# The last pair of experts: both gate-up blocks first, both down blocks second, and the last piece and the prompt outputs in halves

## The reference

```python
def expert_block(args):
    xb, e = args
    h = xb @ w_gu[e] + b_gu[e]
    g = jnp.minimum(h[:, 0::2], SWIGLU_LIMIT)
    up = jnp.clip(h[:, 1::2], -SWIGLU_LIMIT, SWIGLU_LIMIT)
    act = (up + 1.0) * (g * jax.nn.sigmoid(SWIGLU_ALPHA * g))
    return act @ w_dn[e] + b_dn[e]
...
out = jnp.zeros((T + 1, D), x2d.dtype).at[slot_tok].add(ys * slot_gate[:, None])
x = x + f
```

## Time and profile before

| | us |
|---|---|
| median of the runs | 1132.9 |
| profiled execution, its own time | 1134.25 |
| its span, first to last instruction | 1132.3 |
| PE busy | 1076.4 (95%) |
| DVE busy | 323.8 (29%) |
| ACT busy | 152.5 (13%) |
| mean granted clock of PE | 0.977 |

### The profile page before, as it was taken

One profiled execution on the slowest core, in us unless ns is written; L12 is line 12 of the kernel. 1 busy time (PEld: TensorE's weight loads), 2 busy tenths in 40 slices (PEclk: granted clock), 3 DMA queues, 4 the chain that ended last, 5 costly groups with the idle time before them and its releaser, 6 DMA issues.

```text
span 1132.3 us, 12759 instructions
## 1 busy us (share of the span) xinstructions
PE 1076.4 (95%) x4945; PEld 428.5 (38%) x4945; DVE 323.8 (29%) x651; ACT 152.5 (13%) x278; POOL 47.9 (4%) x78
## 2 busy tenths in 40 slices
PE   4999987999999999999999999999999999999996
PEld 3676543333333333333333333333333323333332
DVE  1383438413131313131313131313131221213132
ACT  2143512010101010101010101011110101010100
POOL 4154000000000000000000000000000000000000
PEclk9999977899999999999999999999999999999998
DMA  9905404999999999999999999999999999999991
GB/s 338 376 5 147 175 11 150 359 428 418 427 425 430 427 427 427 429 429 427 428 429 430 426 427 429 430 426 428 430 429 427 428 430 428 427 429 427 428 425 73
DMA packets 32684, 421.51 MB, mean 372 GB/s; under 512 B 4386, under 2 KB 4626, under 8 KB 8062
## 3 DMA queue, kind: packets, MB, share of 16 engines
q1 hardware_dynamic: 31134, 418.08, 88.2%
q0 software_dynamic: 1264, 2.75, 0.7%
q10 hardware_dynamic: 256, 0.26, 0.1%
HBM read 419.81 MB, written 2.33 MB: 373 GB/s over the span
## 4 chain that ended last, share of the span: by engine, by line
PE 74%; DMA 20%; DVE 2%; ACT 2%; issue 1%; SPq 0%; DVEq 0%; ACTq 0%
PE ps L1523 29%; DMA ring<-in_w_gate_up_dram 20%; PE ps L1549 16%; PE ps L1483 9%; PE ps L1171 3%; PE ps L1195 3%; PE ps L1565 3%; PE ps L1531 2%; PE ps L1368 1%; PE ps L1198 1%; PE ps L1500 1%; PE ps L1181 1%; DMA con<-in_const_dram 1%; PE ps L1559 0%; PE ps L1269 0%
## 5 line engine op out<-in xcount | busy, mean ns | idle before, releaser
L1523 PE MATMUL ps<-ring,regA 128*64 128x512 f32 x1536 | 339.2, 595 | 15.0 <-DMA ring<-in_w_gate_up_dram 14.6
L1523 PEld LDWEIGHTS ps<-ring,regA 128*64 128x64 f32 x1536 | 109.8, 137 | 238.7 <-issue 208.8
L1549 PE MATMUL ps<-ring,regA 128*64 128x512 f32 x768 | 174.0, 602 | 0.1
L1121 DVE TENSOR_SCALAR regA<-ps 128x512 f32<-128x512 f32 x32 | 22.1, 692 | 415.8 <-PE ps L1531 415.8
L654 ACT ACTIVATE regA<-regA 128x512 f32<-128x512 f32 x32 | 20.1, 630 | 661.1 <-DVE regA L1121 661.1
L1135 DVE COPY regA<-ps 64x512 f32<-64x512 f32 x64 | 44.1, 689 | 206.5 <-PE ps L1549 205.5
L1483 PE MATMUL ps<-regA 128*128 128x512 f32 (+1 forms) x192 | 97.5, 634 | 2.0 <-DVE regA L1044 2.0
L1549 PEld LDWEIGHTS ps<-ring,regA 128*64 128x64 f32 x768 | 53.2, 138 | 107.2 <-issue 97.7
L1565 PE MATMUL ps<-regA 128*128 128x512 f32 (+1 forms) x136 | 66.6, 613 | 0.0
L1523 PE MATMUL ps<-regX,regA 128*64 128x512 f32 x256 | 57.6, 592 | 0.0
L1523 PE MATMUL ps<-regA 128*64 128x512 f32 x256 | 57.6, 592 | 0.0
(11 more groups left out here) (270 smaller groups left out, 720.3 us busy)
## 6 DMA issues: line engine op xcount, KB each, us to landing
ring<-in_w_gate_up_dram SPq DMA_DIRECT2D x96, 2048.0 KB, 27.9
ring<-in_w_down_dram SPq DMA_DIRECT2D x48, 2048.0 KB, 30.5
regX<-in_w_gate_up_dram SPq DMA_DIRECT2D x16, 2048.0 KB, 26.9
regA<-in_w_gate_up_dram SPq DMA_DIRECT2D x16, 2048.0 KB, 25.7
regA<-in_w_down_dram SPq DMA_DIRECT2D x8, 2048.0 KB, 30.7
regX<-in_w_down_dram SPq DMA_DIRECT2D x8, 2048.0 KB, 32.1
regA<-in_w_in_dram SPq DMA_DIRECT2D x8, 896.0 KB, 14.3
regA<-in_w_out_dram SPq DMA_DIRECT2D x2, 1024.0 KB, 10.5
```

What stands on the lines that cost most here:

```text
L1121: dve.tensor_scalar(g_sb, gu[:, 0::2], LIMIT, None, ALU.min).then_inc(m_g, 1)
L1523: mm = pe.matmul(ps[64 * h:64 * h + 64, 1 + n, :], xT[:, kt, 64 * odd:64 * odd + 64], w[:, c:c + 512], start=(kt == 0), stop=False)
L1549: mm = pe.matmul(ps[64 * n:64 * n + 64, 4, :], actT[:, j, 64 * h:64 * h + 64], w[:, 1024 * j + 512 * n:1024 * j + 512 * n + 512], start=(h ...
```

## The change

In the last pair alone, pieces are loaded and used in another order: the even expert's gate-up (180 to 183), the odd expert's gate-up (184 to 187), the even expert's down (188, 189), the odd expert's down (190, 191). The even expert's down goes to PSUM bank 4 as before; the odd expert's goes to bank 3, and its transposed activation to a tile of its own (`actT_last`, which lies where `g_sb` was). The even expert's result is copied by DVE as soon as its down is done; of the odd expert's result DVE copies one half and ACT the other. The last piece is loaded as two transfers of 1 MB, the second with a semaphore of its own (`s_last`), for which PE waits in the middle of the piece. The two output tiles of `y_prompt` are stored in four halves of 512 columns, each as soon as its add is done. Two semaphores that nobody waited for from another engine are dropped from the list of names.

The diff, cut to its core:

```diff
+        actT_last = g_sb.rearrange("p (j t) -> p j t", j=4)
...
+        LAST_PAIR = [(odd, j) for odd in range(2) for j in range(GU)] + [(odd, GU + h) for odd in range(2) for h in range(2)]
...
-            for i in range(E * PIECES - 2 * SLOTS, E * PIECES):
+            for i in range(E * PIECES - 2 * SLOTS, (E - 2) * PIECES):
                 sp.wait_ge(m_used, i - SLOTS + 1)
                 load_piece(i % SLOTS, i // PIECES, i % PIECES)
+            for i, (odd, j) in enumerate(LAST_PAIR, (E - 2) * PIECES):
+                sp.wait_ge(m_used, i - SLOTS + 1)
+                if i < E * PIECES - 1:
+                    load_piece(i % SLOTS, E - 2 + odd, j)
+                else:
...
+                    sp.dma_start(dst[:, 0:2, :], src[:, 0:2, :]).then_inc(s_slot[i % SLOTS], 16)
+                    sp.dma_start(dst[:, 2:4, :], src[:, 2:4, :]).then_inc(s_last, 16)
...
             for i in range(2):
-                sp.wait_ge(m_add, ADDS * n_over + (done + 6 + 2 * i))
-                sp.sem_inc(sp_passed, 1)
-                sp.dma_start(yp[P * i:P * i + P, :], x_row[:, i, :]).then_inc(s_out, 16)
-            sp.wait_ge(s_out, 16 * 6)
+                for h in range(2):
+                    sp.wait_ge(m_add, ADDS * n_over + (done + 5 + 2 * i + h))
+                    sp.sem_inc(sp_passed, 1)
+                    sp.dma_start(yp[P * i:P * i + P, 512 * h:512 * h + 512],
+                                 x_row[:, i, 512 * h:512 * h + 512]).then_inc(s_out, 16)
+            sp.wait_ge(s_out, 16 * 8)
...
-            pair(PAIRS - 1, False, False)
+            sigmoid(E - 2)
+            copy_act(E - 2)
+            sigmoid(E - 1)
+            copy_act(E - 1, actT_last)
+            act.wait_ge(m_used, PIECES * E)
+            act.activation(y_sb[1][64:128, :], ps[64:128, 3, :], ACT.Copy).then_inc(m_ysb, 1)
...
-            pair(PAIRS - 1, False)
+            activate(E - 2)
+            dve.wait_ge(m_add, ADDS * (PAIRS - 1))
+            add(PAIRS - 1)
+            place_gates(PAIRS - 1)
+            activate(E - 1)
+            dve.wait_ge(m_used, PIECES * E - 2)
+            for n in range(2):
+                dve.tensor_copy(y_sb[n][0:64, :], ps[64 * n:64 * n + 64, 4, :]).then_inc(m_ysb, 1)
+            dve.wait_ge(m_used, PIECES * E)
+            dve.tensor_copy(y_sb[0][64:128, :], ps[0:64, 3, :]).then_inc(m_ysb, 1)
+            dve.wait_ge(m_add, ADDS * PAIRS)
...
+            def down_last(odd, h, lhs, bank):
+
+                w = landed_last(odd, GU + h)
+                for j in range(4):
+                    if odd and h and j == 2:
+                        pe.wait_ge(s_last, 16)
+                    for n in range(2):
+                        mm = pe.matmul(ps[64 * n:64 * n + 64, bank, :], lhs[:, j, 64 * h:64 * h + 64],
+                                       w[:, 1024 * j + 512 * n:1024 * j + 512 * n + 512],
+                                       start=(h == 0 and j == 0), stop=(h == 1 and j == 3))
+                mm.then_inc(m_used, 1)
+
+            def pair_last():
...
+                act_transposes(p * 2)
+                place_half(gated, y_sb, 1, 1).then_inc(m_pl, 1)
+                gate_up(p, 0, 1, False, True)
+                pe.wait_ge(m_aT, p * 2 + 1)
+                pe.wait_ge(m_add, p * ADDS + 4)
+                down_last(0, 0, actT, 4)
+                act_transposes(p * 2 + 1)
+                down_last(0, 1, actT, 4)
+                pe.wait_ge(m_aT, p * 2 + 2)
+                down_last(1, 0, actT_last, 3)
+                down_last(1, 1, actT_last, 3)
...
-            pair(PAIRS - 1, PAIRS // 2 - 1, 2, False)
+            pair_last()
```

More of the change, by code:

```diff
@@ L169, in hybrid_layer, with at_last @@
         slot = [ring[:, s, :] for s in range(6)] + [regA[:, tail - PIECE:tail], regX[:, 0:PIECE]]
+        LAST_PAIR = [(odd, j) for odd in range(2) for j in range(GU)] + [(odd, GU + h) for odd in range(2) for h in range(2)]
+        def at_last(odd, j):
+            return divmod(2 * PIECES + LAST_PAIR.index((odd, j)), SLOTS)
         def at(x, j):
@@ L216, in hybrid_layer @@
         s_zero = sem("zeroed")
+        s_last = sem("last_half_piece_landed")
         s_dve, s_act, s_pool = sem("dve_step"), sem("act_step"), sem("pool_step")
@@ L222, in hybrid_layer @@
                  "sc_t", "sc_cp", "sc_tr", "s_rd", "s_neg", "s_exp", "s_pn", "s_ptr", "s_pcp", "s_pv",
-                 "h_last", "kr_tr", "krow_cp", "st_tr", "st_cp", "out_a", "xmid_a", "out_r", "xq_in", "xq", "xq_tr",
+                 "kr_tr", "krow_cp", "st_tr", "st_cp", "out_a", "xmid_a", "out_r", "xq_in", "xq", "xq_tr",
                  "xq_cp", "xs_rows", "xmid", "wr_g", "ss_f", "ms_f", "rstd_f", "xn",
-                 "xnt_tr", "xnt_cp", "xnt_cp2", "logit", "topd", "tope", "mask", "posd", "placed", "ovd", "gt_tr", "gt_cp")
+                 "xnt_tr", "xnt_cp", "xnt_cp2", "logit", "topd", "tope", "mask", "posd", "ovd", "gt_tr", "gt_cp")
         S = {n: sem(n) for n in names}
@@ L654, in sigmoid, with copy_act @@
                 act.activation(sig_sb, g_sb, ACT.Sigmoid, scale=ALPHA).then_inc(m_sig, 1)
-            def copy_act(q):
+            def copy_act(q, dst=actT):
                 act.wait_ge(m_atr, q + 1)
-                act.activation(actT[:, :, :], ps[:, 3, :].rearrange("p (j t) -> p j t", j=4),
+                act.activation(dst[:, :, :], ps[:, 3, :].rearrange("p (j t) -> p j t", j=4),
                                ACT.Copy).then_inc(m_aT, 1)
@@ L911, in _ @@
             then(dve.tensor_tensor(hs[:, :, NP_:T], rT[:, :, NP_:T], vec[:, :, R_H0:R_H0 + NS], ALU.mult))
-            then(dve.tensor_tensor(hs[:, :, NP_:T], hs[:, :, NP_:T], uT[:, :, NP_:T], ALU.add), "h_last")
+            then(dve.tensor_tensor(hs[:, :, NP_:T], hs[:, :, NP_:T], uT[:, :, NP_:T], ALU.add))
             dve.wait_ge(S["gelu"], 1)
@@ L1008, in places @@
                 then(dve.scalar_tensor_tensor(out=place_cols[r, i, 0:E], in0=ps[r, CBANK[i], 0:E],
-                                              scalar=float(POS0), in1=msk[r, i, :], op0=ALU.add, op1=ALU.mult), "placed")
+                                              scalar=float(POS0), in1=msk[r, i, :], op0=ALU.add, op1=ALU.mult))
             add_r(0, 0, 1)
@@ L1512, in landed, with landed_last, gate_up @@
                 return slot[s]
-            def gate_up(p, r, x, over):
+            def landed_last(odd, j):
+                again, s = at_last(odd, j)
+                pe.wait_ge(s_slot[s], (E // 4 - 1) * 48 + (16 * again + 16))
+                return slot[s]
+            def gate_up(p, r, x, over, last=False):
                 odd = x % 2
@@ L1518, in gate_up @@
                     if kt % 2 == 0:
-                        w = landed(r, x, kt // 2, over)
+                        w = landed_last(odd, kt // 2) if last else landed(r, x, kt // 2, over)
                     for n in range(2):
@@ L1602, in pair @@
                 down(p, r, x + 1, over, ahead)
+            def down_last(odd, h, lhs, bank):
[9 more added lines that the diff above has]
+            def pair_last():
+                p = PAIRS - 1
+                pe.wait_ge(m_xT, p * 2 + 2)
+                gate_up(p, 0, 0, False, True)
+                pe.wait_ge(m_ysb, p * 4)
+                pe.wait_ge(m_gated, p * 2)
+                pe.wait_ge(m_idx, p + 1)
+                place_quarters(gated, y_sb)
+                place_half(gated, y_sb, 0, 0)
+                place_half(gated, y_sb, 0, 1).then_inc(m_pl, 1)
+                place_half(gated, y_sb, 1, 0)
+                act_transposes(p * 2)
[9 more added lines that the diff above has]
+                down_last(1, 1, actT_last, 3)
             def gather_first(g):
```

2 lines of the change are left out of this document (added).

## The result

The changed kernel takes 1128.66 us (median of 6, 1127.07 to 1128.95), the one before beside it 1133.45 (median of 6, 1132.42 to 1136.16): a ratio of 0.995 [0.994, 0.996], faster by about half a per cent. Timed twice more it gave 1129.04 beside 1135.08 (0.995 [0.9937, 0.9962]) and 1128.17 beside 1134.65 (0.9946 [0.993, 0.9963]), so the medians differ by 4.8, 6.0 and 6.5 us. The forecast was 1127.0, a gain of 6.0, with a range from 1124.9 to 1129.0; 1128.66 lies near the range's upper end.

A forecast was written before the change was run, and what follows sets the result against it. The prediction took full DMA engines moving weights as the bound, leaving only work behind the last piece to shorten. 5.65 plus 0.35 made 6.0 off 1132.9, so 1126.9, stated as 1127.0 us; range 1124.9 to 1129.0.

The forecast's parts named there:

- Landings: Loads at the end: the last pieces land as before, piece 190 at 1108.4 and piece 191 at 1113.1 us.
- Products: Last down on PE: 32 products at full clock take 7.09 from 1108.4 to 1115.5, 6.4 us less than 1121.94.
- The branch: PE's branch past the overflow loop, uncovered behind the last half piece: 3.49 us, delaying placing and taking back 1.5.
- Rival A: Branch past the overflow loop stays covered: placing begins at 1116.45, 1.5 more gained, 1125.4 us; chance 0.22.
- The clock: PE's clock in the 2.5 us pause before placing: cost between 0 and 1.83 us, taken as 0.
- 1.5 as a rival: Rival B: branch uncovered and clock falls in the pause, placing largely at half clock; 1.5 us, 1128.5; chance 0.28.
- The last piece in halves: Last load as two transfers with 8 KB rows: between nothing and 1.2 us later, taken as 0.
- The stores: Halved final stores on SP: 0.35 us of gain, ends -0.2 and 0.6.
- The sum: Whole tail: 5.65 from products and copies less the branch, plus 0.35 from stores, gives 6.0 us.

The follow-up runs named there:

- short skip: Changed kernel with the body of TensorE's overflow loop left out, so the branch's target lies nearer; 1127.23 us, ratio 0.9941 to the kernel before.

## Why the prediction was right

**Landings: right.** Forecast 1108.4 and 1113.1; measured 1107.65 and 1112.56. They are 0.75 and 0.54 early. SP had issued both pieces 0.68 earlier than in the profile before (1074.42 and 1077.86, beside the earlier trace rows), before any product of the change, so this is the scatter of the runs. (The last issue, of piece 191, waits for piece 183, as the prediction has it: a slot is free when the piece eight before it has been used, not seven.)

**Products: right.** The last down was to end 2.4 behind the last landing, at full clock; it ended 2.32 behind.

**The branch: right, and shown.** Load 0.1 behind the last half piece's landing, branch 0.95 behind it, 3.49 long, and placing 0.3 behind its end were expected; measured were 0.06, 0.93, 3.39 and 0.37. Leaving out the loop's body takes the branch to 0.23 (from 3.73 beside it), and putting the placing ahead takes it off the path. Rival A (covered) needs a sequencer that runs ahead of the landing, and it did not. As I had put it, the branch would take back 1.5; the short skip gives 1.3 to 1.6 from landing to end.

**The clock: undecided as forecast.** I took 0, with 1.5 as a rival (0.40 against 0.28); it is 0 in two profiles of the changed kernel, and in one 1.7 on the products and 1.2 on the span.

**The last piece in halves: right in its cost, too kind in its use.** 4.91 us from 1107.65 to 1112.56 against 4.81 before, so a loss of 0.1 at most. What it could gain stayed hidden behind the branch (it is about 1.4 once the branch is out of the way).

**The stores: mis-sized.** "I take 0.35 of gain"; it was 0.05. Half of the bytes behind the last add did not come off the end, as the spread of the two bounds had allowed.

**The sum.** 6.0 expected. In the profiles 5.80 came from landing to end and 0.61 from an earlier landing, which is no part of the change; that the two together come near the forecast is in part luck. The other two profiles of the changed kernel give 4.30 and 5.49 from landing to end, against the same 19.16. Between medians it was 4.8, 6.0 and 6.5. The first median lies 1.7 above the forecast: 0.55 of it is that the kernel before came out at 1133.45 and not at 1132.9, and 0.3 the stores. The rest isn't taken apart by any run; it is within what the clock (1.2 in an execution), a branch of 3.7 instead of 3.4 and the scatter of the landings move.

## What to carry to other kernels

When a change shortens the tail of a kernel, look for what the sequencer does there: a branch or a load that lay hidden behind products is laid bare, and its row stands in the trace of the kernel before. Put the path that is always taken ahead of the branch past the path that rarely is; here that took 0.8 us off the time from the last landing to the end (13.36 to 12.53). And moving such a branch ahead is no help where the queue is a few microseconds deep: it then stops the engine sooner, and costs the clock too.

## What the runs showed of the hardware that I had not expected

- A taken branch whose target had to be fetched took 3.39 to 3.73 us with the DMA engines all but idle, 4.77 in two profiles, with two packets of instructions in each instead of one, and 6.59 beside weight traffic at 0.97, where the packet came 4.1 us behind the branch instead of 1.04. With nothing to fetch it took 0.23 forward and 0.21 back over two pairs of experts, and 0.08 where not taken.
- With a packet of instructions among the last stores, from the last add to the end it took 3.76 to 3.97; without one 3.09 to 3.39, and 2.62 in the execution whose clock fell in the placing.
- Pauses of 2.37, 2.57, 2.61 and 2.63 us ahead of the same products: the clock fell behind the second and the third and not behind the others.
